# The second feed-forward's norm split in two: the gain in the matmul's operand, the token's factor on every up product

## The chip, the cores and the metric

The kernel runs on one core of a Trainium2 chip. The time is the device time of one execution in microseconds (us), lower being better. TensorE is PE in the profile, VectorE DVE, ScalarE ACT, GpSimd POOL, SyncE SP.

## The reference, cut to what matters

Two transformer blocks run one after the other on 256 tokens of width 1024, all in float32. The change touches only the end of the second one, its feed-forward on the residual `x`:

```python
def rms_norm(x, g):            # x / sqrt(mean(x*x) + eps) * g
...
h = rms_norm(x, norm_ffn_g[l])
u = causal_dwconv(h @ ffn_up[l], ffn_conv_w[l], ffn_conv_b[l])   # 3 taps along the tokens
u_gate, u_val = jnp.split(u, 2, axis=-1)                        # 2 x 2816 columns
x = x + (jax.nn.gelu(u_gate) * u_val) @ ffn_down[l]
return rms_norm(x, final_norm_g)
```

## The kernel before

Activations lie transposed: the 1024 features are 8 chunks `k` of 128 partitions, the 256 tokens lie along the free axis. So a gain (one number per feature) is a per-partition scalar, and a norm's factor (one number per token) is a row along the free axis, held on all partitions in `rstd`.

**Weights** stream as tiles of 128x1024 through a ring of four slots. For matmuls in parts, ScalarE copies each half tile (512 columns) rounded to the matmul's type into `w_parts` ("hi", the helper `tile_hi`, L1245), and VectorE subtracts that from the tile to get the rest ("lo", `part_lo`, L2249). A product is then three passes, hi*hi, hi*lo, lo*hi. `w_parts` holds four half tiles, so the hi of a half waits until TensorE has used the half four places earlier. SyncE loads the tile four places on once the lo of a tile is written.

**The output projection before the feed-forward** is 8 plain matmul tiles (L731), each followed on VectorE by the addition into `res` (L2243, semaphore `resid`) and on ScalarE by its square (L1487).

**The norm.** TensorE then sums the squares over the partitions with a matrix of ones (L741), ScalarE takes the root (L1045), VectorE the reciprocal (L1579, `inverse`) and scales all eight chunks by gain and factor into `h4T` (L1877, `norm`). ScalarE and VectorE split `h4T` into `h_parts` hi and lo, two chunks at a time (L1375, L2044). While this goes on TensorE turns the residual (L981) into the banks in which the down products accumulate later, and then waits for `h_lo`.

**The feed-forward** has 22 steps `f`, one for each 128 rows of the gate half and of the value half. On TensorE a step is `ffn_up(f)`, two products of 24 matmuls each (m = 0 gate, m = 1 value, L997), into banks 4 to 7 by turns, and `ffn_down(f - 1)` (12 matmuls, L1009). ScalarE reads a finished product from the bank, multiplies it by the last tap and adds the bias, each a per-partition scalar (`up_out`, L1508); VectorE adds the other two taps from the bank (`ff_taps`, L2264 and L2267), the second waiting for the first by a semaphore; ScalarE applies gelu (L1513); VectorE multiplies gate by value (`ff_gate`, L2273); ScalarE and VectorE split that (L1518 `act_parts`, L2278 `ff_lo`) for the down product. All engines run their programs strictly in the written order. The steps 2 to 17 run in a loop with registers on ScalarE and VectorE, four steps to an iteration; steps 1 and 18 to 21 are written out. A step of VectorE (before) is: gate(f-1), lo, lo, ff_lo(f-1), taps(f,0), lo, lo, taps(f,1), lo, lo. A step of ScalarE (`ff_step`) is:

```python
used(x, 0, i4); ahead(x, 0, i4)
used(x, 1, i4); act_parts(f - 1, i4); up_out(f, 0, i4); ahead(x, 1, i4)
used(x + 1, 0, i4); ahead(x + 1, 0, i4)
used(x + 1, 1, i4); up_out(f, 1, i4); ahead(x + 1, 1, i4); ff_gelu(f, i4)
used(x + 2, 0, i4); ahead(x + 2, 0, i4)
used(x + 2, 1, i4); ahead(x + 2, 1, i4)
```

Here `x = 3f - 1` is the tile of the gate product, x + 1 that of the value product, x + 2 that of down(f-1); `used(x, half)` waits until TensorE has used that half, and `ahead(x, half)` makes the hi of the same half of tile x + 2.

Of the kernel before, what the change touches and what calls it, by code (L numbers as in the profile page):

```python
# [14 lines left out]
F32 = mybir.dt.float32  # L15
F32R = mybir.dt.float32r
U32 = mybir.dt.uint32
ALU = mybir.AluOpType
# [53 lines left out]
rgw_in rg_in rg_conv_done rg_gates rg_sig rg_coeff rg_mult rg_ln rg_steps h3_ready rg_exp rg_pow rg_square lam_exp  # L72
logits2 probs2 maps2 o2_stat o2_root o2_ready ff_out ff_conv ff_taps ff_gelu ff_act final_done""".split()


def build(nc, wstream, x_t, cols_in, mats_in, mats1_in, matsa_in, crow_in, rows_in, out):
    ctx = ExitStack()
    with ctx:
# [215 lines left out]
        y2T = buf("y2T", KT, S)  # L294
        h4T = buf("h4T", KT, S)
        upp = buf("upp", 2, 2, S + 2)
        upc = buf("upc", 2, 2, S)
# [83 lines left out]
        def _(pe):  # L381
# [592 lines left out]
            for d in range(KT):  # L974
                full(N_OUT2 + d, y2T, 4 + d % 4, (sem["resid"], 2 * KT + d - 3) if d >= 4 else None)
            sum_squares2(4, sq3, 3)
            for tt in range(2):
                for d in range(KT):
                    if 2 * tt + d // 4 == 3:
                        pe.wait_ge(sem["roots"], 5)  # L980
                    pe.matmul(ps[:, 2 * tt + d // 4, P * (d % 4):P * (d % 4) + P], res[:, d, P * tt:P * tt + P], ident,  # L981
                              start=(d % 4 == 0), stop=False, is_transpose=True, skip_group_check=True)
            pe.wait_ge(sem["h_lo"], 16)

            def ffn_up(f, i4=0):

                for m in range(2):
                    if f >= 2:  # L990
                        pe.wait_ge(sem["ff_conv"], 2 * i4 + 2 * f - 3 + m)
                    x = max(3 * f - 1, 0) + m
                    for half in range(2):
                        pe.wait_ge(sem["w_lo"], 6 * i4 + 2 * (M_FFN + x) + half + 1)
                        for k in range(4):
                            for c, e in PASSES:
                                mm = pe.matmul(ps[:, 4 + 2 * (f % 2) + m, 0:S], w_parts[:, c, (2 * (M_FFN + x) + half) % 4, P * k:P * k + P],  # L997
                                               h_parts[:, e, 4 * half + k, :], start=(half == 0 and k == 0 and c + e == 0),
                                               stop=(half == 1 and k == 3 and c == 1))
                        mm.then_inc(sem["tiles_done" if half else "half_used"], 1)  # L1000

# [11 lines left out]

            ffn_up(0)
            ffn_up(1)
            ffn_down(0)
            with pe.Fori(0, (FT - 2) // 4) as i:
                for f in range(2, 6):
                    ffn_up(f, 4 * i)
                    ffn_down(f - 1, 4 * i)  # L1020
# [3 lines left out]
        def _(act):  # L1024
# [347 lines left out]

            def act_hi(src):
                for c in range(4):
                    act.activation(h_parts[:, 0, 2 * c:2 * c + 2, :], src[:, 2 * c:2 * c + 2, :], ACT.Copy).then_inc(sem["h_hi"], 1)  # L1375

            for k in range(KT):
# [113 lines left out]

            def used(x, half, i4=0):
# [68 lines left out]
        def _(dve):  # L1561
# [311 lines left out]

            def norm(r, dst, src, gain):
                inverse(r, S)
                for k in range(KT):
                    o = dve.scalar_tensor_tensor(dst[:, k, :], src[:, k, :], gain[:, k:k + 1], rstd[:, 0:S], ALU.mult, ALU.mult)  # L1877
                return o

            def route_query(h):  # L1880
# [158 lines left out]
            step(127, last=True)  # L2039
            def dve_lo(r, src):  # L2040

                for c in range(4):
                    dve.wait_ge(sem["h_hi"], 4 * r + c + 5)
                    dve.tensor_tensor(h_parts[:, 1, 2 * c:2 * c + 2, :], src[:, 2 * c:2 * c + 2, :],  # L2044
                                      h_parts[:, 0, 2 * c:2 * c + 2, :].bitcast(F32), ALU.subtract).then_inc(sem["h_lo"], 1)

            def in2_lo(t, half):
# [184 lines left out]
            for d in range(KT):  # L2232
                dve.wait_ge(sem["tiles_done"], N_BR2 + 2 * d + 2)
                b = 2 * (d % 2)
                y, t = y2T[:, d, :], fft[:, d % 2, :]
                dve.tensor_tensor(t, ps[:, b, 0:S], g2T[:, d, :], ALU.mult)
                link(dve.tensor_tensor(y, ps[:, b, S:2 * S], g2T[:, 16 + d, :], ALU.mult))
                link(dve.tensor_tensor(y, y, t, ALU.add))
                link(dve.tensor_tensor(t, ps[:, b + 1, 0:S], g2T[:, 8 + d, :], ALU.mult))
                dve.tensor_tensor(y, y, t, ALU.add).then_inc(sem["merged"], 1)  # L2240
            for d in range(KT):
                dve.wait_ge(sem["tiles_done"], N_OUT2 + d + 1)
                dve.tensor_tensor(res[:, d, :], ps[:, 4 + d % 4, 0:S], x2T[:, d, :], ALU.add).then_inc(sem["resid"], 1)  # L2243
            def part_lo(x, i4=0):

                for half in range(2):
                    h = 2 * (M_FFN + x) + half
                    dve.wait_ge(sem["w_hi"], 6 * i4 + h + 1)
                    dve.tensor_tensor(w_parts[:, 1, h % 4, :], ring[:, tile_of(M_FFN + x) % RING, 512 * half:512 * half + 512],  # L2249
                                      w_parts[:, 0, h % 4, :].bitcast(F32), ALU.subtract).then_inc(sem["w_lo"], 1)  # L2250

            for x in range(2):
                part_lo(x)
            norm(4, h4T, res, col("norm_ffn2")).then_inc(sem["normed"], 1)
            dve_lo(2, h4T)

            taps3 = col("ff_conv", 44, 3)

            def ff_taps(f, m, i4=0):

                bk, c = 4 + 2 * (f % 2) + m, bass.ds(i4 + f + FT * m, 1)
                dst = upc[:, f % 2, m, :]
                dve.wait_ge(sem["ff_out"], 2 * i4 + 2 * f + m + 1)
                dve.scalar_tensor_tensor(dst[:, 1:S], ps[:, bk, 0:S - 1], taps3[:, c, 1], dst[:, 1:S], ALU.mult, ALU.add  # L2264
                                         ).then_inc(sem["ff_taps"], 1)
                dve.wait_ge(sem["ff_taps"], 2 * i4 + 2 * f + m + 1)
                dve.scalar_tensor_tensor(dst[:, 2:S], ps[:, bk, 0:S - 2], taps3[:, c, 0], dst[:, 2:S], ALU.mult, ALU.add  # L2267
                                         ).then_inc(sem["ff_conv"], 1)
# [12 lines left out]
            def ff_step(f, i4=0):  # L2281

                ff_gate(f - 1, i4)
                part_lo(3 * f + 1, i4)
                ff_lo(f - 1, i4)
                ff_taps(f, 0, i4)
                part_lo(3 * f + 2, i4)
                ff_taps(f, 1, i4)
                if 3 * f + 3 < 3 * FT:
                    part_lo(3 * f + 3, i4)  # L2290

            for m in range(2):
                part_lo(2 + m)
                ff_taps(0, m)
# [220 lines left out]
```

## Time and profile before

| | us |
|---|---|
| median of 3 runs (lowest, highest) | 1961.96 (1959.88, 1962.26) |
| the profiled execution, its own time | 1961.08 |
| its span in the trace | 1959.3 |
| TensorE busy | 1828.5 (93%) |
| VectorE busy | 1232.5 (63%) |
| ScalarE busy | 993.5 (51%) |

The span runs from the first to the last instruction; what lies around it is 1.8 us. All times below are counted from the span's start. The stage that the change touches runs from about 1744.9 us (last projection tile through) to the end.

### The profile page before, as it was taken

The page shows a single profiled execution, that of the slowest core. Times are in us where ns is not written, and L with a number is a line of the kernel's source. Part 1 is how long each engine was busy: PE and PEld are TensorE (multiplying, and loading weights), DVE is VectorE, ACT ScalarE, POOL GpSimd, SP SyncE. Part 2 cuts the span into 40 slices and gives each one's busy share as a digit, 9 for nine tenths or more (in the row PEclk, how much of TensorE's full clock was granted, in tenths as well). Part 3 has the DMA queues.
Part 4 walks back from the last instruction along what each step waited for, and adds up shares of the span by engine and source line. Part 5 has one row for each costly group of instructions (what it writes and reads, how often), then busy time and mean ns, then how long its engine had stood idle before and what let it go on. Part 6 is the DMA issues. An engine that isn't in the chain of part 4 may idle for free.

```text
span 1959.3 us, 34312 instructions
## 1 busy us (share of the span) xinstructions
PE 1828.5 (93%) x11798; PEld 1639.1 (84%) x11798; DVE 1232.5 (63%) x2463; ACT 993.5 (51%) x1986; POOL 148.7 (8%) x118
## 2 busy tenths in 40 slices
PE   7899989998999986799999999999899997989997
PEld 1777879998889976688899999999899886879997
DVE  1685356555178979866666666666776664237776
ACT  2545523241136668766555555555558555016665
POOL 0000003330044720000000000000000000000000
PEclk9899969898999999999999999999999998999999
DMA  7423212122445530155555555555354432435553
GB/s 263 176 99 98 93 59 97 65 74 99 150 152 173 181 127 1 36 192 194 190 192 182 187 187 187 188 183 192 138 178 158 147 112 82 154 129 180 182 182 120
DMA packets 77267, 283.28 MB, mean 145 GB/s; under 512 B 8576, under 2 KB 8576, under 8 KB 76928
## 3 DMA queue, kind: packets, MB, share of 16 engines
q1 hardware_dynamic: 77184, 282.16, 42.2%
q8 instruction: 53, 0.87, 0.2%
q14 instruction: 30, 0.25, 0.0%
HBM read 281.08 MB, written 1.05 MB: 144 GB/s over the span
## 4 chain that ended last, share of the span: by engine, by line
PE 83%; DVE 11%; ACT 4%; issue 1%; DMA 1%; POOL 1%; POOLq 0%; SPq 0%; DVEq 0%; ACTq 0%
PE banks L802 18%; PE banks L790 16%; PE banks L864 8%; PE banks L427 7%; PE banks L997 6%; PE banks L731 4%; PE banks L1009 3%; PE banks L602 2%; PE banks L586 2%; DVE split L1979 2%; PE banks L969 1%; PE banks L754 1%; DVE arena L1977 1%; PE banks L400 1%; PE banks L591 1%
## 5 line engine op out<-in xcount | busy, mean ns | idle before, releaser
L1264 ACT ACTIVATE split<-arena 128x512 fp32r<-128x512 f32 x508 | 318.9, 629 | 145.4 <-PE banks L790 83.1
L790 PEld LDWEIGHTS banks<-split 128*128 128x128 f32 x3072 | 379.5, 192 | 11.1 <-DVE split L1916 3.1
L790 PE MATMUL banks<-split 128*128 128x256 f32 x3072 | 383.0, 283 | 3.1 <-DVE split L1916 2.2
L802 PE MATMUL banks<-split 128*128 128x512 f32 x1536 | 363.4, 390 | 2.7 <-issue 2.7
L1993 DVE TENSOR_TENSOR split<-arena,split 128x512 fp32r<-128x512 f32 x412 | 281.8, 690 | 115.8 <-ACT split L1264 110.1
L802 PEld LDWEIGHTS banks<-split 128*128 128x128 f32 x1536 | 283.3, 188 | 58.4 <-issue 2.9
L1245 ACT ACTIVATE split<-arena 128x512 fp32r<-128x512 f32 x264 | 163.9, 626 | 84.8 <-PE banks L864 29.8
L864 PE MATMUL banks<-split 128*128 128x256 f32 x1344 | 169.3, 286 | 4.0 <-DVE split L2075 3.9
L864 PEld LDWEIGHTS banks<-split 128*128 128x128 f32 x1344 | 164.7, 193 | 7.6 <-issue 5.9
L427 PE MATMUL banks<-split 128*128 128x256 f32 (+2 forms) x936 | 155.1, 329 | 7.5 <-DVE split L1585 6.5
L427 PEld LDWEIGHTS banks<-split 128*128 128x128 f32 (+1 forms) x936 | 138.4, 202 | 25.9 <-issue 8.3
L997 PEld LDWEIGHTS banks<-split 128*128 128x128 f32 x1056 | 131.1, 194 | 8.9 <-DVE split L2044 7.3
L997 PE MATMUL banks<-split 128*128 128x256 f32 x1056 | 131.7, 285 | 7.1 <-DVE split L2044 7.1
L2052 DVE TENSOR_TENSOR split<-arena,split 128x512 fp32r<-128x512 f32 x128 | 87.2, 689 | 70.6 <-ACT split L1245 69.2
L2249 DVE TENSOR_TENSOR split<-arena,split 128x512 fp32r<-128x512 f32 x132 | 89.1, 688 | 46.8 <-ACT split L1245 45.2
L828 PE MATMUL banks<-split,arena 128*128 128x128 f32 x512 | 66.1, 284 | 32.3 <-DVE arena L1982 32.3
L2377 POOL TENSOR_TENSOR split<-arena,split 128x512 fp32r<-128x512 f32 x68 | 90.7, 1362 | 71.9 <-DVE split L1916 51.2
L828 PEld LDWEIGHTS banks<-split,arena 128*128 128x128 f32 x512 | 61.1, 196 | 37.4 <-DVE split L1979 33.4
L731 PE MATMUL banks<-arena 128*128 128x256 f32 x384 | 84.7, 380 | 3.7 <-DVE arena L2240 2.2
L1585 DVE TENSOR_TENSOR split<-arena,split 128x512 fp32r<-128x512 f32 x78 | 53.1, 690 | 54.2 <-ACT split L1052 53.8
L731 PEld LDWEIGHTS banks<-arena 128*128 128x128 f32 x384 | 72.8, 190 | 14.3 <-DVE arena L2240 2.6
L2009 DVE TENSOR_TENSOR arena<-arena 128x256 f32<-128x256 f32 x80 | 49.1, 614 | 45.0 <-ACT arena L1326 44.9
(372 smaller groups left out, 2384.1 us busy)
## 6 DMA issues: line engine op xcount, KB each, us to landing
arena<-wstream SPq DMA_DIRECT2D x525, 512.0 KB, 3.2
arena<-x_t SPq DMA_DIRECT2D x1, 2048.0 KB, 13.4
arena<-matsa SPq DMA_DIRECT2D x1, 1234.0 KB, 6.3
out_t<-arena SPq DMA_DIRECT2D x4, 256.0 KB, 2.1
arena<-mats SPq DMA_DIRECT2D x1, 576.0 KB, 8.0
arena<-crow SPq DMA_DIRECT2D x1, 512.0 KB, 7.1
arena<-rows SPq DMA_DIRECT2D x1, 512.0 KB, 4.4
arena<-mats SPq DMA_DIRECT2D x1, 449.0 KB, 5.5
```

What stands on the lines that cost most here:

```text
L427: mm = pe.matmul(ps[0:rows, b, 0:m], w_parts[:, c, (2 * t + k // 4) % 4, P * (k % 4):P * (k % 4) + rows], hp[:, e, k, 0:m], start=(k == 0 ...
L731: mm = pe.matmul(ps[:, b, 0:S], w[:, P * k:P * k + P], src[:, k, :], start=(k == 0), stop=(k == KT - 1))
L790: mm = pe.matmul(ps[:, 4 + b, 0:S], w_parts[:, c, (2 * m + half) % 4, P * k:P * k + P], h_parts[:, e, 4 * half + k, :], start=(half == 0 a ...
L802: mm = pe.matmul(ps[:, 2 * tt + half, :], g_parts[:, e, j % 2, P * tt:P * tt + P], w_parts[:, c, (2 * m + half) % 4, :], start=(first and ...
L828: pe.matmul(ps[:, W_BANKS[g % 3] + t // 4, P * (t % 4):P * (t % 4) + P], hot1[g % 2][:, t, :], hot2[:, g % 2, t, :].bitcast(F32), start=Tr ...
L864: mm = pe.matmul(out, w_parts[:, c, (2 * m + half) % 4, P * k:P * k + P], src[:, e, 4 * half + k, :], start=(half == 0 and k == 0 and c + ...
L997: mm = pe.matmul(ps[:, 4 + 2 * (f % 2) + m, 0:S], w_parts[:, c, (2 * (M_FFN + x) + half) % 4, P * k:P * k + P], h_parts[:, e, 4 * half + k ...
L1245: act.activation(w_parts[:, 0, h % 4, :], ring[:, slot, 512 * half:512 * half + 512], ACT.Copy).then_inc(sem["w_hi"], 1)
L1264: act.activation(w_parts[:, 0, (2 * m + half) % 4, :], ring[:, peer_slot(m), 512 * half:512 * half + 512], ACT.Copy).then_inc(sem["w_hi"], 1)
L1993: dve.tensor_tensor(w_parts[:, 1, (2 * m + half) % 4, :], ring[:, slot, 512 * half:512 * half + 512], w_parts[:, 0, (2 * m + half) % 4, :] ...
L2249: dve.tensor_tensor(w_parts[:, 1, h % 4, :], ring[:, tile_of(M_FFN + x) % RING, 512 * half:512 * half + 512], w_parts[:, 0, h % 4, :].bitc ...
L2377: pool.tensor_tensor(w_parts[:, 1, (2 * m + half) % 4, :], ring[:, (N_PEER + m) % RING, 512 * half:512 * half + 512], w_parts[:, 0, (2 * m ...
```

## The change: what it does

The gain is put into the matmul's operand without waiting for the factor, chunk by chunk as the residual is made: ScalarE writes hi = `res * gain` into `h_parts` (an Identity activation with the gain as scale), VectorE writes lo = `res * gain - hi` (`weighted_lo`). `h4T`, `norm`, `act_hi` and `dve_lo` are gone. The factor, which is the same for all features of a token, is put on each finished up product by a new VectorE operation `ff_norm`, from the bank into a buffer `upn`; `up_out` and both taps read `upn` in place of the bank. `up_out` now waits for `ff_norm`, and TensorE's reuse of a bank waits for `ff_norm` of two steps back rather than for the taps. TensorE's order becomes: first up product, sums of squares, second up product, turning of the residual, both products of step 1.

```diff
# TensorE
-            sum_squares2(4, sq3, 3)
-            for tt in range(2):
+            def turn_residual(tt):
...
-            pe.wait_ge(sem["h_lo"], 16)
...
+            def ffn_up(f, m, i4=0):
+                if f >= 2:
+                    pe.wait_ge(sem["ff_norm"], 2 * i4 + 2 * f - 3 + m)
+                x = max(3 * f - 1, 0) + m
+                if x == 0:
+                    pe.wait_ge(sem["resid"], 2 * KT + 5)
+                for half in range(2):
+                    pe.wait_ge(sem["w_lo"], 6 * i4 + 2 * (M_FFN + x) + half + 1)
+                    for k in range(4):
+                        if x == 0:
+                            pe.wait_ge(sem["h_lo"], 12 + 4 * half + k + 1)
...
-            ffn_up(0)
-            ffn_up(1)
+            ffn_up(0, 0)
+            sum_squares2(4, sq3, 3)
+            ffn_up(0, 1)
+            for tt in range(2):
+                turn_residual(tt)
+            for m in range(2):
+                ffn_up(1, m)
# ScalarE
                 act.wait_ge(sem["resid"], 2 * KT + k + 1)
+                act.activation(h_parts[:, 0, k, :], res[:, k, :], ACT.Identity, scale=col("norm_ffn2")[:, k:k + 1]).then_inc(sem["h_hi"], 1)
                 act.activation(sq3[:, k, :], res[:, k, :], ACT.Square).then_inc(sem["squares"], 1)
-            roots(4, S, 3)
-            act.wait_ge(sem["normed"], 2)
-            act_hi(h4T)
...
                 c = bass.ds(i4 + f + FT * m, 1)
-                act.activation(upc[:, f % 2, m, :], ps[:, 4 + 2 * (f % 2) + m, 0:S], ACT.Identity, scale=last_tap[:, c],
+                act.wait_ge(sem["ff_norm"], 2 * i4 + 2 * f + m + 1)
+                act.activation(upc[:, f % 2, m, :], upn[:, f % 2, m, :], ACT.Identity, scale=last_tap[:, c],
                                bias=col("ff_conv_b")[:, c]).then_inc(sem["ff_out"], 1)
...
             for x in range(2):
                 for half in range(2):
                     used(x, half)
-                    if half:
-                        up_out(0, x)
                     ahead(x, half)
+                if x == 0:
+                    roots(4, S, 3)
+            for m in range(2):
+                up_out(0, m)
             ff_gelu(0)
# VectorE
+            def weighted_lo(k):
+                dve.wait_ge(sem["h_hi"], 12 + k + 1)
+                dve.scalar_tensor_tensor(h_parts[:, 1, k, :], res[:, k, :], col("norm_ffn2")[:, k:k + 1], h_parts[:, 0, k, :].bitcast(F32),
+                                         ALU.mult, ALU.subtract).then_inc(sem["h_lo"], 1)
             for d in range(KT):
                 dve.wait_ge(sem["tiles_done"], N_OUT2 + d + 1)
                 dve.tensor_tensor(res[:, d, :], ps[:, 4 + d % 4, 0:S], x2T[:, d, :], ALU.add).then_inc(sem["resid"], 1)
+                if d:
+                    weighted_lo(d - 1)
+                if d == 6:
+                    for half in range(2):
+                        part_lo(0, half)
+            weighted_lo(KT - 1)
+            for x in (1, 2):
                 for half in range(2):
+                    part_lo(x, half)
+            inverse(4, S)
...
-            norm(4, h4T, res, col("norm_ffn2")).then_inc(sem["normed"], 1)
-            dve_lo(2, h4T)
...
+            def ff_norm(f, m, i4=0):
+                dve.wait_ge(sem["tiles_done"], 3 * i4 + N_FFN + max(3 * f - 1, 0) + m + 1)
+                dve.tensor_tensor(upn[:, f % 2, m, :], ps[:, 4 + 2 * (f % 2) + m, 0:S], rstd[:, 0:S], ALU.mult).then_inc(sem["ff_norm"], 1)
...
             def ff_step(f, i4=0):
                 ff_gate(f - 1, i4)
-                part_lo(3 * f + 1, i4)
+                part_lo(3 * f + 1, 0, i4)
+                ff_norm(f, 0, i4)
                 ff_lo(f - 1, i4)
+                part_lo(3 * f + 1, 1, i4)
                 ff_taps(f, 0, i4)
-                part_lo(3 * f + 2, i4)
+                part_lo(3 * f + 2, 0, i4)
+                ff_norm(f, 1, i4)
+                part_lo(3 * f + 2, 1, i4)
                 ff_taps(f, 1, i4)
                 if 3 * f + 3 < 3 * FT:
-                    part_lo(3 * f + 3, i4)
+                    for half in range(2):
+                        part_lo(3 * f + 3, half, i4)
 
             for m in range(2):
-                part_lo(2 + m)
+                ff_norm(0, m)
+            for half in range(2):
+                part_lo(3, half)
+            for m in range(2):
                 ff_taps(0, m)
```

## Rows read from the trace of the kernel before

**Rows 1.** The page: busy times, and the chain that ended last by engine.
```profile
PE 1828.5 (93%) x11798; PEld 1639.1 (84%) x11798; DVE 1232.5 (63%) x2463; ACT 993.5 (51%) x1986; POOL 148.7 (8%) x118
PE 83%; DVE 11%; ACT 4%; issue 1%; DMA 1%; POOL 1%; POOLq 0%; SPq 0%; DVEq 0%; ACTq 0%
```
**Rows 2.** Windows: stretch, us, busy PE, PEld, DVE, ACT, POOL, PE clock, DMA, GB/s.
```profile
1773.98:1911.09 137.11, 137.11 (x963) 129.06 (x962) 100.54 (x192) 83.07 (x160) 0.00 (x0) 1.00 0.54 184
1748.00:1757.30 9.30, 2.23 (x19) 1.89 (x17) 7.51 (x13) 2.66 (x5) 0.00 (x0) 0.85 0.45 162
1757.30:1761.30 4.00, 3.99 (x18) 3.99 (x19) 0.36 (x1) 0.63 (x1) 0.00 (x0) 0.50 0.00 0
740.00:800.00 60.00, 40.74 (x323) 37.32 (x321) 60.00 (x101) 49.36 (x143) 0.00 (x0) 1.00 0.00 1
```
**Rows 3.** The chain that ended last, in order of time: start us, us, what.
```profile
1745.02 3.47 PE banks L741 x16
...
1749.02 1.76 DVE arena L1579
...
1750.81 3.27 DVE arena L1877 x8
...
1754.76 2.51 DVE split L2044 x4
...
1757.31 7.76 PE banks L997 x48
...
1773.98 5.75 PE banks L997 x48
1779.73 2.84 PE banks L1009 x12
...
1842.56 5.75 PE banks L997 x48
...
1936.62 5.77 PE banks L997 x48
...
1946.71 3.07 PE banks L1009 x12
```
**Rows 4.** Timeline of a loop step on ACT: start us, us, operation [idle before].
```profile
1848.56 0.57 ACT L1508 ACTIVATE arena<-banks,arena 128x256 f32<-128x256 f32 x1 [1.02 <-PE banks L997]
1849.03 0.62 ACT L1245 ACTIVATE split<-arena 128x512 fp32r<-128x512 f32 x1
...
1852.59 0.63 ACT L1245 ACTIVATE split<-arena 128x512 fp32r<-128x512 f32 x1 [0.80 <-PE banks L997]
```
**Rows 5.** The same timeline on DVE.
```profile
1850.29 0.48 DVE L2264 SCALAR_TENSOR_TENSOR arena<-banks,arena 128x255 f32<-128x255 f32 x1
1850.91 0.48 DVE L2267 SCALAR_TENSOR_TENSOR arena<-banks,arena 128x254 f32<-128x254 f32 x1
1851.31 1.28 DVE L2249 TENSOR_TENSOR split<-arena,split 128x512 fp32r<-128x512 f32 x2
1852.51 0.42 DVE L2273 TENSOR_TENSOR arena<-arena 128x256 f32<-128x256 f32 x1
1853.26 0.69 DVE L2249 TENSOR_TENSOR split<-arena,split 128x512 fp32r<-128x512 f32 x1 [0.33 <-ACT split L1245]
```
**Rows 6.** Groups by line and shape: line, engine, tiles, count | busy us, mean ns | idle before.
```profile
L1508 ACT ACTIVATE arena<-banks,arena 128x256 f32<-128x256 f32 x44 | 24.5, 557 | 21.8 <-PE banks L997 21.8
L1402 ACT ACTIVATE arena<-banks,arena 128x256 f32<-128x256 f32 x24 | 11.3, 472 | 20.6 <-PE banks L864 20.6
L1487 ACT ACTIVATE arena<-arena 128x256 f32<-128x256 f32 x8 | 3.3, 416 | 81.2 <-DVE arena L2243 81.2
L1235 ACT ACTIVATE arena<-arena 128x256 f32<-128x256 f32 x8 | 4.1, 508 | 58.0 <-DVE arena L1871 58.0
L2243 DVE TENSOR_TENSOR arena<-banks,arena 128x256 f32<-128x256 f32 x8 | 3.4, 425 | 25.0 <-PE banks L731 25.0
L1877 DVE SCALAR_TENSOR_TENSOR arena<-arena 128x256 f32<-128x256 f32 x8 | 3.3, 480 | 0.0
```

More of the change, by code:

```diff
@@ L72 @@
 rgw_in rg_in rg_conv_done rg_gates rg_sig rg_coeff rg_mult rg_ln rg_steps h3_ready rg_exp rg_pow rg_square lam_exp
-logits2 probs2 maps2 o2_stat o2_root o2_ready ff_out ff_conv ff_taps ff_gelu ff_act final_done""".split()
+logits2 probs2 maps2 o2_stat o2_root o2_ready ff_norm ff_out ff_conv ff_taps ff_gelu ff_act final_done""".split()
 def build(nc, wstream, x_t, cols_in, mats_in, mats1_in, matsa_in, crow_in, rows_in, out):
@@ L294, in build @@
         y2T = buf("y2T", KT, S)
-        h4T = buf("h4T", KT, S)
-        upp = buf("upp", 2, 2, S + 2)
+        upn = buf("upn", 2, 2, S)
         upc = buf("upc", 2, 2, S)
@@ L982, in _ @@
                               start=(d % 4 == 0), stop=False, is_transpose=True, skip_group_check=True)
-            pe.wait_ge(sem["h_lo"], 16)
[L987 to L1000, printed above, removed]
+            def ffn_up(f, m, i4=0):
[9 more added lines that the diff above has]
+                            pe.wait_ge(sem["h_lo"], 12 + 4 * half + k + 1)
+                        for c, e in PASSES:
+                            mm = pe.matmul(ps[:, 4 + 2 * (f % 2) + m, 0:S], w_parts[:, c, (2 * (M_FFN + x) + half) % 4, P * k:P * k + P],
+                                           h_parts[:, e, 4 * half + k, :], start=(half == 0 and k == 0 and c + e == 0),
+                                           stop=(half == 1 and k == 3 and c == 1))
+                    mm.then_inc(sem["tiles_done" if half else "half_used"], 1)
             def ffn_down(f, i4=0, x=None, last=False):
@@ L1018, in _ @@
                 for f in range(2, 6):
-                    ffn_up(f, 4 * i)
+                    for m in range(2):
+                        ffn_up(f, m, 4 * i)
                     ffn_down(f - 1, 4 * i)
@@ L1371, in part_hi @@
                 tile_hi(n % RING, 12 * i4 + 16 * (n // RING + 1), half, 2 * m + half)
-            def act_hi(src):
-                for c in range(4):
-                    act.activation(h_parts[:, 0, 2 * c:2 * c + 2, :], src[:, 2 * c:2 * c + 2, :], ACT.Copy).then_inc(sem["h_hi"], 1)
             for k in range(KT):
@@ L1872, in _ @@
                                          ALU.mult, ALU.add).then_inc(sem["resid"], 1)
[L1874 to L1878, printed above, removed]
             def route_query(h):
@@ L2039, in _ @@
             step(127, last=True)
[L2040 to L2045, printed above, removed]
             def in2_lo(t, half):
@@ L2240, in _, with part_lo @@
                 dve.tensor_tensor(y, y, t, ALU.add).then_inc(sem["merged"], 1)
+            def part_lo(x, half, i4=0):
+                h = 2 * (M_FFN + x) + half
+                dve.wait_ge(sem["w_hi"], 6 * i4 + h + 1)
+                dve.tensor_tensor(w_parts[:, 1, h % 4, :], ring[:, tile_of(M_FFN + x) % RING, 512 * half:512 * half + 512],
+                                  w_parts[:, 0, h % 4, :].bitcast(F32), ALU.subtract).then_inc(sem["w_lo"], 1)
+            def weighted_lo(k):
+                dve.wait_ge(sem["h_hi"], 12 + k + 1)
+                dve.scalar_tensor_tensor(h_parts[:, 1, k, :], res[:, k, :], col("norm_ffn2")[:, k:k + 1], h_parts[:, 0, k, :].bitcast(F32),
+                                         ALU.mult, ALU.subtract).then_inc(sem["h_lo"], 1)
             for d in range(KT):
@@ L2243, in _ @@
                 dve.tensor_tensor(res[:, d, :], ps[:, 4 + d % 4, 0:S], x2T[:, d, :], ALU.add).then_inc(sem["resid"], 1)
-            def part_lo(x, i4=0):
-                for half in range(2):
[L2247 to L2250, printed above, removed]
@@ L2252, in _ @@
-            for x in range(2):
-                part_lo(x)
-            norm(4, h4T, res, col("norm_ffn2")).then_inc(sem["normed"], 1)
-            dve_lo(2, h4T)
+                if d:
[5 more added lines that the diff above has]
+            for x in (1, 2):
+                for half in range(2):
+                    part_lo(x, half)
+            inverse(4, S)
@@ L2257, in _ @@
             taps3 = col("ff_conv", 44, 3)
+            def ff_norm(f, m, i4=0):
+                dve.wait_ge(sem["tiles_done"], 3 * i4 + N_FFN + max(3 * f - 1, 0) + m + 1)
+                dve.tensor_tensor(upn[:, f % 2, m, :], ps[:, 4 + 2 * (f % 2) + m, 0:S], rstd[:, 0:S], ALU.mult).then_inc(sem["ff_norm"], 1)
             def ff_taps(f, m, i4=0):
-                bk, c = 4 + 2 * (f % 2) + m, bass.ds(i4 + f + FT * m, 1)
-                dst = upc[:, f % 2, m, :]
+                c = bass.ds(i4 + f + FT * m, 1)
+                src, dst = upn[:, f % 2, m, :], upc[:, f % 2, m, :]
@@ L2263, in ff_taps @@
                 dve.wait_ge(sem["ff_out"], 2 * i4 + 2 * f + m + 1)
-                dve.scalar_tensor_tensor(dst[:, 1:S], ps[:, bk, 0:S - 1], taps3[:, c, 1], dst[:, 1:S], ALU.mult, ALU.add
+                dve.scalar_tensor_tensor(dst[:, 1:S], src[:, 0:S - 1], taps3[:, c, 1], dst[:, 1:S], ALU.mult, ALU.add
                                          ).then_inc(sem["ff_taps"], 1)
                 dve.wait_ge(sem["ff_taps"], 2 * i4 + 2 * f + m + 1)
-                dve.scalar_tensor_tensor(dst[:, 2:S], ps[:, bk, 0:S - 2], taps3[:, c, 0], dst[:, 2:S], ALU.mult, ALU.add
+                dve.scalar_tensor_tensor(dst[:, 2:S], src[:, 0:S - 2], taps3[:, c, 0], dst[:, 2:S], ALU.mult, ALU.add
@@ L2283, in ff_step @@
                 ff_gate(f - 1, i4)
-                part_lo(3 * f + 1, i4)
+                part_lo(3 * f + 1, 0, i4)
+                ff_norm(f, 0, i4)
                 ff_lo(f - 1, i4)
+                part_lo(3 * f + 1, 1, i4)
                 ff_taps(f, 0, i4)
-                part_lo(3 * f + 2, i4)
+                part_lo(3 * f + 2, 0, i4)
+                ff_norm(f, 1, i4)
+                part_lo(3 * f + 2, 1, i4)
                 ff_taps(f, 1, i4)
                 if 3 * f + 3 < 3 * FT:
-                    part_lo(3 * f + 3, i4)
+                    for half in range(2):
+                        part_lo(3 * f + 3, half, i4)
             for m in range(2):
-                part_lo(2 + m)
+                ff_norm(0, m)
+            for half in range(2):
+                part_lo(3, half)
+            for m in range(2):
                 ff_taps(0, m)
```

## The prediction

> **What bounds the kernel now.** I read the page first: TensorE is busy 93% of the span, and the chain of waits that ended last is TensorE for 83% [rows 1]. So time is won only where TensorE stands still, and lost only where something makes it stand still. Then I looked at the feed-forward by windows and along the chain. Two stretches differ. In the first, from 1748.0 to 1757.3 us, TensorE is busy 2.23 of 9.30 us, and behind it runs at a granted clock of 0.50 [rows 2], that is at 1.2 in place of 2.4 GHz. The chain leaves it in this stretch: root, reciprocal (1.76 us), eight scalings (3.27), splits (2.51) [rows 3]. In the second, the loop, TensorE is busy 137.11 of 137.11 us at clock 1.00, and the chain is nothing but up products (5.75 us) and down products (2.8 us); 16 steps take 137.11 us, 8.57 each. VectorE is busy 100.54 us there (73%), ScalarE 83.07 (61%) [rows 2, 3]. The change takes work out of the first stretch and puts work on the two other engines in the second.
>
> **Part 1, the start.** TensorE's idle time of 9.30 - 2.23 = 7.07 us goes, since the first up product needs only residual chunks, each split a few tenths after it is made. Will they be there? The last chunk is added by 1745.5; hi (0.51) and lo (0.48) follow, done by 1746.5; TensorE starts the product at 1744.9 and reaches that chunk 2.5 us later. The sums then come 2.87 us later than before, reciprocal included until 1753.7, and two up products, the sums and the turning (some 11 us) cover them. With the idle time goes the slow clock behind it: from 1757.31 to 1773.98 the chain has four products and a down product, which at the loop's pace are 4 x 2.875 + 2.83 = 14.33 us and took 16.67 [rows 3], so 2.3 us more. Laid out in the new order, TensorE begins step 2 at 1764.7 in place of 1773.98: **9.3 us gained**. The extra ScalarE and VectorE operations per projection tile (1 each, about 0.5 us in a period of 3.4) hide under its matmuls, and the loads keep their order: SyncE's next load waits for a lo that is now made earlier, and POOL's queue has nothing in this stage.
>
> **Part 2, the loop.** Counted by busy time nothing happens: ff_norm is a tensor-tensor from a bank, 0.425 us as L2243 [rows 6]; two per step bring VectorE from 6.28 to 7.13 of 8.57 us. But busy time is not what decides here. ff_norm stands ahead of up_out, up_out stands in ScalarE's order ahead of a hi, and VectorE's own next operation is the lo of that hi. Both engines work in order, so twice per step VectorE stands still through a round trip over ScalarE. Before, up_out waited only for TensorE, and the lo's had slack. So I add the ring in which each operation can only start when the one before allows:
>
> - ff_norm 0.425, up to its end [rows 6].
> - From there to up_out. In the loop this operation computes its scalar addresses from registers after its wait: the product of step 10 ends on the chain at 1842.56 + 5.75 = 1848.31 and up_out starts at 1848.56, 0.25 later; in the written-out step 21 the product ends at 1942.39 and the chain goes on 0.02 later [rows 3, 4]. I take 0.26.
> - up_out itself, as far as it holds up the next operation. Bounds: 0.32 to 0.51. From a bank it takes 0.557 with two scalars (scale and bias), L1402 with one takes 0.472; out of SBUF no scalar takes 0.416 (L1487) and one takes 0.508 (L1235) [rows 6]. So a scalar costs 0.09, SBUF as source 0.036 more than a bank, and two scalars out of SBUF come to 0.60. The next operation starts 0.10 ahead of the end (1848.56 to 1849.03 at 0.57) [rows 4]: 0.51, the value nearest in form. The low end is the row without scalars.
> - hi 0.62, and 0.03 until the lo starts (1852.59 + 0.63 to 1853.26) [rows 4, 5].
>
> One round trip is 1.85, two are 3.69. The rest of the ring is VectorE's own work, start to start: six lo's at 0.60 (two L2249 from 1851.31 to 1852.51) = 3.62; twice the first tap to the second, 0.62 (1850.29 to 1850.91), = 1.24; twice the second tap, 0.40, = 0.80; the gate, 0.34 (its 0.42 less the 0.08 by which the others overlap) [rows 5]. ff_lo lies inside the wait for the hi. **The ring is 9.69 us against 8.57.** The taps read SBUF now. Bounds for one: 0.42, which is what L2273 takes on SBUF alone in another operation [rows 5], and the 0.48 of today. I leave them at 0.48, since L1877 is the same operation on SBUF alone and takes 0.480 [rows 6].
>
> The Trainium skill says otherwise on that point: "VectorE: DVE Perf Modes", section on the TRN2 errata, gives VectorE 58 cycles plus the elements at 0.96 GHz out of SBUF and 120 out of PSUM, so a tap would be some 65 ns cheaper, an estimate from that page. By it the ring would be 9.43; the trace, with 480 ns from either side, does not agree.
>
> In the written-out steps 18 to 21 there is no register work: 0.23 less per round trip and about 0.1 less per pair of taps, a ring of 9.02, still over TensorE's 8.5.
>
> **The sum.** I lay the operations out one by one with these durations. Gate of step 0 falls at 1757.8; step 1's ring and a short wait for its product put gate 1 at 1767.15. At that time VectorE still has slack: TensorE needs its step 2 from 1764.7 on and the splits are two half tiles ahead; this is used up within two steps, after which TensorE waits about 1.1 us per step for a lo. Gate 17 is at 1767.15 + 16 x 9.69 = 1922.2, gate 20 at +3 x 9.02 = 1949.3. Gate 21 follows after 9.02 less the two lo's of a tile that does not exist (1.2), then gate, hi and lo of the gated product (0.42 each, 0.2 between) and the down product, 3.07 [rows 3]: last matmul at 1961.6. Before it is 1946.71 + 3.07 = 1949.78 [rows 3]. The rest (final norm, output) is unchanged. **Sum: +11.8 us**, being -9.3 at the start, about +18 in the steps and +3 at the tail, where TensorE now waits longer for the last gated product. On the profiled execution's own 1961.08 that is 1972.9. That execution lies between the lowest and highest of the three runs and 0.9 below their median, so I take 1973.
>
> **The rivals.**
> B, the register work is done ahead of the wait. For: sequencers do some of it early elsewhere. Against: the 0.25 us before up_out, where the wait comes first, as it would here. The ring is 9.24 and the end 7 us earlier: 1966.
> C, the taps get cheaper once they leave the bank, down to the low end: 0.06 each, four per step, 0.24 off the ring, 20 steps, 5 us less: 1968. For: a bank is a different source, and ScalarE shows 0.036 between the two. Against: L1877 [rows 6]. The rule of the Trainium skill above is this rival.
> D, the other side, faster: TensorE stays the bound. Place: the two round trips of the loop. It decides for this when the ring is under 8.57, that is, if the round trips overlap VectorE's own work rather than follow it, which leaves the 7.13 of busy time. For: 73% plus 10% occupancy. Against: program order; the lo right behind each round trip cannot be made earlier, and only ff_lo is between. Then the start's gain stays, less some 0.8 at the tail: 1961.08 - 9.3 + 0.8 = 1952.6.
> M, a mixture: low ends throughout (up_out at 0.33, part of the register work hidden) give a ring near 9.1: between 1958 and 1965, no change that can be told.
> E, the clock falls in TensorE's new pauses. The clock fell once behind an idle stretch of 7 us, but from 740 to 800 us TensorE is busy only 68% and keeps 1.00 [rows 2], and pauses here are 1.1 us at a time. Each fall like the one at the start costs about 2.3 us; two to four of them give 1978 to 1982.
> G, the change does not do what it says: the first product still waits for the last chunk or a load. All of part 1 except a little is gone: 1980.
>
> **How the numbers follow.** The forecast 0.60, B 0.10, C 0.06, D 0.09, M 0.05, E 0.08, G 0.02. The range from 1965 to 1979 takes in the forecast with its bounds (ring 9.55 to 9.85, 3 us each way), B, C and half of E; D, M, G and the rest of E, 0.2, are outside. A measurement of this kernel tells 0.2% (3.9 us) from no change. Faster: D, 0.09. Within: M, 0.05. Slower: the rest, 0.86.
>
> **What would show it.** Right: no idle time of TensorE and no clock below 1.00 between 1745 and 1765, step 2 begins near 1764.7; in the loop, steps of 9.7 us with TensorE waiting about 1.1 us for a lo and VectorE twice about 1.2 us for ScalarE's hi; up_out at 0.60. Steps of 9.2 to 9.5 mean B or C (look at the time from ff_norm's end to up_out, and at the taps' duration). Wrong altogether: steps of 8.57 with no wait on lo, or clock stretches at 0.50 inside the loop, or TensorE idle before its first up product.

## The result and the profile after

The changed kernel takes 1975.16 us (median of 6 runs, 1968.87 to 1979.09) against 1962.03 before (6 runs, 1959.44 to 1965.45). The ratio is 1.0064, 95% interval 1.0046 to 1.0082: slower by 0.6%. Forecast: 1973, range 1965 to 1979.

The profiled execution took 1979.09 us, its span is 1977.0. It is 18 us above the profiled one of before, but 4.4 us of that lie in front of the stage that was changed: its first matmul starts at 1749.23 instead of 1744.86. Up to there TensorE runs the same program in both kernels. The gap between the same matmul groups is 1.3 us at 214 us of before's time, 5.2 at 313, and 4.5 from 383 us on; at the stage's start it is 4.4, so the operations added to each projection tile cost nothing. It comes with the granted clock: in the first 320 us the changed kernel's execution has it at half speed for 61.5 us, that of before for 51.3 (added up from the trace in windows of 4 us). I therefore compare **the stage**, from its first matmul behind the projection to the end of the last one: 1749.23 to 1967.46, that is 218.2 us, against 204.9 before. That is +13.3; forecast +11.8.

The start, in the timeline of the changed kernel (start us, us, engine, line, operation, count, idle before):

```profile
1749.23 3.21 PE L995 MATMUL banks<-split 128*128 128x256 f32 x24
...
1752.28 3.62 PE L740 MATMUL banks<-arena 128*128 128x256 f32 x16
...
1755.55 3.23 PE L995 MATMUL banks<-split 128*128 128x256 f32 x24
...
1758.61 1.91 PE L979 MATMUL banks<-arena 128*128 128x128 f32 x16
...
1760.28 6.00 PE L995 MATMUL banks<-split 128*128 128x256 f32 x48
...
1766.12 2.91 PE L1007 MATMUL banks<-split 128*128 128x512 f32 x12
...
1768.86 5.92 PE L995 MATMUL banks<-split 128*128 128x256 f32 x48
```

One matmul group follows the other without idle time. Step 2 starts 1768.86 - 1749.23 = 19.63 us into the stage; before it was 1773.82 - 1744.86 = 28.96, so 9.3 us are gained. The windows say the same of the clock, which was 0.50 behind the idle stretch of before [rows 2], and show the price in the loop (columns as in [rows 2]):

```profile
1749.20:1768.86 19.66, 19.66 (x142) 18.73 (x141) 13.76 (x26) 10.26 (x19) 0.00 (x0) 1.00 0.56 189
1788.84:1922.00 133.16, 123.88 (x831) 111.64 (x832) 95.70 (x195) 69.00 (x137) 0.00 (x0) 1.00 0.49 164
1958.60:1962.80 4.20, 0.14 (x1) 0.00 (x0) 2.42 (x5) 1.76 (x4) 0.00 (x0) 1.00 0.00 0
1963.80:1967.40 3.60, 3.60 (x10) 2.38 (x8) 0.00 (x0) 0.00 (x0) 0.00 (x0) 0.53 0.00 0
```

In the loop TensorE is now busy 123.88 of 133.16 us where it had no idle time, and VectorE, at 72%, is not busy all the time either. So neither engine is full: the time goes into waits in a circle. One step of it, VectorE first, then ScalarE:

```profile
1781.28 0.42 DVE L2275 TENSOR_TENSOR arena<-arena 128x256 f32<-128x256 f32 x1
1781.61 0.68 DVE L2232 TENSOR_TENSOR split<-arena,split 128x512 fp32r<-128x512 f32 x1
...
1782.21 0.42 DVE L2259 TENSOR_TENSOR arena<-banks,arena 128x256 f32<-128x256 f32 x1
1782.55 0.41 DVE L2280 TENSOR_TENSOR split<-arena,split 128x256 fp32r<-128x256 f32 x1
...
1784.04 0.69 DVE L2232 TENSOR_TENSOR split<-arena,split 128x512 fp32r<-128x512 f32 x1 [1.07 <-ACT split L1249]
...
1786.27 0.42 DVE L2259 TENSOR_TENSOR arena<-banks,arena 128x256 f32<-128x256 f32 x1
1786.54 1.59 PE L995 MATMUL banks<-split 128*128 128x256 f32 x12
...
1788.09 0.69 DVE L2232 TENSOR_TENSOR split<-arena,split 128x512 fp32r<-128x512 f32 x1 [1.40 <-ACT split L1249]
...
1788.84 4.77 PE L995 MATMUL banks<-split 128*128 128x256 f32 x36 [0.71 <-DVE split L2232]
...
1790.93 0.42 DVE L2275 TENSOR_TENSOR arena<-arena 128x256 f32<-128x256 f32 x1
```
```profile
1782.88 0.60 ACT L1506 ACTIVATE arena<-arena 128x256 f32<-128x256 f32 x1 [0.73 <-DVE arena L2259]
1783.39 1.14 ACT L1249 ACTIVATE split<-arena 128x512 fp32r<-128x512 f32 x2
1786.94 0.60 ACT L1506 ACTIVATE arena<-arena 128x256 f32<-128x256 f32 x1 [2.41 <-PE banks L1007]
1787.44 0.62 ACT L1249 ACTIVATE split<-arena 128x512 fp32r<-128x512 f32 x1
```

Follow the round trip: ff_norm (L2259) ends at 1786.27 + 0.42 = 1786.69; up_out (L1506) starts 0.25 later; the hi behind it (L1249) 0.50 after that; VectorE's lo (L2232) starts at 1788.09, having waited 1.40 us; TensorE has waited for that lo too. From gate (L2275) to gate it is 1790.93 - 1781.28 = 9.65 us. That is 1.15 us more than 8.50, TensorE's own time for a step; 0.71 of it shows as idle time in front of L995, the other 0.44 is in the records on both sides of that wait, which take 1.59 and 4.77 us for 48 matmuls where step 2 takes 5.92. A caution on reading: the second up_out names "PE banks L1007" as what ended its wait. That is the releaser the profile inferred; the down product merely ended at about the same time. The first up_out, in the same place of the program, names L2259, and the 0.25 us behind ff_norm's end are the same both times.

### The profile page after: what moved, and what is told of

It reads as the page before. It is cut to its first block, busy times and chain, and to the rows that moved or that the text cites. A ratio compares the mean times of both kernels' runs of the same rounds, so it can differ in the third digit from the quotient of the medians.

```text
span 1977.0 us, 34413 instructions
## 1 busy us (share of the span) xinstructions
PE 1837.3 (93%) x11798; PEld 1641.4 (83%) x11798; DVE 1243.3 (63%) x2503; ACT 993.1 (50%) x1990; POOL 148.8 (8%) x118
## 4 chain that ended last, share of the span: by engine, by line
PE 74%; DVE 15%; ACT 5%; issue 4%; DMA 1%; POOL 1%; DVEq 0%; ACTq 0%; POOLq 0%; SPq 0%
PE banks L801 18%; PE banks L789 16%; PE banks L863 8%; PE banks L426 7%; PE banks L730 4%; PE banks L601 2%; DVE split L2232 2%; PE banks L585 2%; DVE split L1973 2%; ACT split L1249 2%; PE banks L968 1%; PE banks L753 1%; DVE arena L1971 1%; PE banks L399 1%; DVE arena L2266 1%
## 5 line engine op out<-in xcount | busy, mean ns | idle before, releaser
L1268 ACT ACTIVATE split<-arena 128x512 fp32r<-128x512 f32 x508 | 319.4, 630 | 145.1 <-PE banks L789 83.1
L789 PE MATMUL banks<-split 128*128 128x256 f32 x3072 | 383.0, 283 | 3.2 <-DVE split L1910 2.3
L1249 ACT ACTIVATE split<-arena 128x512 fp32r<-128x512 f32 x264 | 157.5, 622 | 53.0 <-PE banks L863 29.7
L863 PE MATMUL banks<-split 128*128 128x256 f32 x1344 | 169.3, 286 | 4.0 <-DVE split L2062 3.9
L995 PE MATMUL banks<-split 128*128 128x256 f32 x1056 | 138.8, 286 | 11.7 <-DVE split L2232 11.7
L995 PEld LDWEIGHTS banks<-split 128*128 128x128 f32 x1056 | 130.7, 191 | 20.3 <-DVE split L2232 15.5
L2232 DVE TENSOR_TENSOR split<-arena,split 128x512 fp32r<-128x512 f32 x132 | 88.8, 688 | 50.3 <-ACT split L1249 50.3
## 6 DMA issues: line engine op xcount, KB each, us to landing
arena<-x_t SPq DMA_DIRECT2D x1, 2048.0 KB, 13.1
```

Of the source, the lines that this page charges most:

```text
L789: mm = pe.matmul(ps[:, 4 + b, 0:S], w_parts[:, c, (2 * m + half) % 4, P * k:P * k + P], h_parts[:, e, 4 * half + k, :], start=(half == 0 a ...
L863: mm = pe.matmul(out, w_parts[:, c, (2 * m + half) % 4, P * k:P * k + P], src[:, e, 4 * half + k, :], start=(half == 0 and k == 0 and c + ...
L1249: act.activation(w_parts[:, 0, h % 4, :], ring[:, slot, 512 * half:512 * half + 512], ACT.Copy).then_inc(sem["w_hi"], 1)
L1268: act.activation(w_parts[:, 0, (2 * m + half) % 4, :], ring[:, peer_slot(m), 512 * half:512 * half + 512], ACT.Copy).then_inc(sem["w_hi"], 1)
```

## The experiments

All rest on the changed kernel unless said otherwise. "Steps" is the distance between the starts of the down products of neighbouring loop steps. Experiment 1 has seven executions; each of the others has one, so they are compared by the steps and the stage of that execution, which stay clear of what happens to the clock before the stage. A table of all runs closes the section.

**1. The hi in front of up_out.**

```diff
                 act_parts(f - 1, i4)
+                ahead(x, 1, i4)
                 up_out(f, 0, i4)
-                ahead(x, 1, i4)
...
+                ahead(x + 1, 1, i4)
                 up_out(f, 1, i4)
-                ahead(x + 1, 1, i4)
```

> Edit: the changed kernel, with one line moved twice on ScalarE: the hi of the next half tile (ahead) stands in front of up_out instead of behind it, for the gate and for the value product. No instruction more or less. Theory 1 (the ring: VectorE waits twice per step for a hi that stands in ScalarE's order behind up_out, which waits for ff_norm): the ring is broken, steps go back to TensorE's 8.57 us from 9.65, the start's gain of 9.3 us stays, and the time is about 9 us below before, near 1952 (ratio to before 0.995). Theory 2 (VectorE's and ScalarE's added work, or contention for the memory, is what slows the steps): the same work is done, so steps stay within 0.1 us of 9.65 and the time near 1974. Theory 3 (the register work and semaphore traffic of the added waits on TensorE's side): steps stay at 9.65 as well.

Measured: 1950.94 us (median of 7 runs, 1945.04 to 1957.33) against 1961.6 of before beside it (12 runs); ratio 0.9945, interval 0.9924 to 0.9967. The timeline of TensorE's down products and the windows:

```profile
1866.82 2.91 PE L1007 MATMUL banks<-split 128*128 128x512 f32 x12
...
1875.32 2.91 PE L1007 MATMUL banks<-split 128*128 128x512 f32 x12
```
```profile
1764.00:1900.00 136.00, 136.00 (x963) 128.14 (x962) 115.02 (x225) 85.55 (x161) 0.00 (x0) 1.00 0.55 185
```

Steps are 8.50 us (why not 8.57, see experiment 9), TensorE has no idle time, and VectorE is busy 85% where it was 72%. The same instructions in another order: theory 1 holds, 2 and 3 fall. The stage takes 194.0 us, 24.2 less than the changed kernel and 10.9 less than before. This is the version that beats both kernels.

**2 and 3. Two spare products on VectorE, inside the waits or outside them.** The operation is the same in both kernels, `dve.tensor_tensor(spare, rstd[:, 0:S], rstd[:, 0:S], ALU.mult)`.

```diff
# 2: in the waits
                 ff_lo(f - 1, i4)
+                spare product
...
                 ff_norm(f, 1, i4)
+                spare product
# 3: behind the taps
                 ff_taps(f, 0, i4)
+                spare product
...
                 ff_taps(f, 1, i4)
+                spare product
```

> Edit: the changed kernel plus two spare VectorE products of 128x256 per step (0.42 us each), one behind ff_lo and one behind the second ff_norm, that is at the places where VectorE waits for ScalarE's hi. Theory 1 (the ring) says that they fall into waits of some 1.1 and 1.4 us: steps stay at 9.65 us (within 0.03). Theory 2 (VectorE's amount of work decides) says at least 2 x 0.34 more: steps of 10.3 us, 11 us more in the time.

> Edit: the same two spare VectorE products per step, but behind the two pairs of taps, where VectorE does not wait. Theory 1 (the ring) says they lengthen it by 2 x 0.34: steps of 10.33 us, some 14 us over the 20 steps. Theory 2 (the amount of work) says the same as for the kernel with the spare products in the waits; the two kernels have the same instructions, so a difference between them is the place alone.

Down products of two neighbouring steps, first with the products in the waits, then behind the taps:

```profile
1867.92 2.91 PE L1008 MATMUL banks<-split 128*128 128x512 f32 x12
...
1877.58 2.91 PE L1008 MATMUL banks<-split 128*128 128x512 f32 x12
```
```profile
1867.46 2.91 PE L1008 MATMUL banks<-split 128*128 128x512 f32 x12
...
1877.78 2.91 PE L1008 MATMUL banks<-split 128*128 128x512 f32 x12
```

9.66 against 10.32 us: in the waits the same work is free, on the ring it costs 0.67 per step, twice its start-to-start time of 0.33. The stages are 217.9 and 232.3 us (changed kernel 218.2): -0.4 and +14.1. With the same instructions in both kernels, it is their place that costs and not their amount.

**4. The same with the ring broken.** Kernel 1 with the spare products where kernel 3 has them.

> Edit: the kernel with hi first, plus the two spare VectorE products of 128x256 per step behind the taps, where they cost 0.67 us per step in the changed kernel. Theory 1 (only the ring made VectorE's order decide): with the ring broken VectorE's own work, about 7.1 us, leaves 1.4 us of slack per step, the two products (0.67) fit and steps stay at 8.50 us. Theory 2 (amount of work decides as soon as it grows): steps of 9.2 us.

```profile
1868.78 2.91 PE L1008 MATMUL banks<-split 128*128 128x512 f32 x12
...
1877.28 2.91 PE L1008 MATMUL banks<-split 128*128 128x512 f32 x12
```

8.50 us; the stage takes 194.5. From 1790 to 1910 us VectorE is busy 108.34 of 120 us (90%) and TensorE all 120. What cost 14 us in experiment 3 is free here.

**5. Only the value product's hi in front.** The second of the two moves of experiment 1 alone.

> Edit: the changed kernel with the hi in front of up_out for the value product alone; the gate product's round trip stays. The ring theory with one round trip in place of two: the ring is below TensorE's own time (9.65 less about 1.2), steps of 8.50 to 8.65 us. A theory in which each wait costs by itself, whatever else the engines do, says half of the loss stays: about 9.1 us.

The first seven distances are 8.50, the eighth 8.54, while VectorE's lead lasts; then they settle at 8.66 (down products at 1862.38, 1871.04 and 1879.71); the stage takes 197.7. That is a touch over the upper end of what the ring theory gave, and far from 9.1. The rows tell why 8.66: with the hi out of the way VectorE's next wait is for up_out itself, whose end lets the taps start.

```profile
1856.21 0.41 DVE L2259 TENSOR_TENSOR arena<-banks,arena 128x256 f32<-128x256 f32 x1
1856.54 0.68 DVE L2232 TENSOR_TENSOR split<-arena,split 128x512 fp32r<-128x512 f32 x1
1857.64 0.48 DVE L2266 SCALAR_TENSOR_TENSOR arena<-arena 128x255 f32<-128x255 f32 x1 [0.42 <-ACT arena L1506]
```

From ff_norm to the first tap it is 1.43 us; in the changed kernel it is 1788.70 - 1786.27 = 2.43 (the round trip and a lo). 9.65 - 1.00 = 8.65. With both moved it would be some 7.65 (an estimate from these rows), which is below TensorE's 8.50.

**6. Loops written out.**

```diff
-            with act.Fori(0, (FT - 2) // 4 - 1) as i:
-                for f in range(2, 6):
-                    ff_step(f, 4 * i)
-            for f in range(FT - 4, FT):
+            for f in range(2, FT):
                 ff_step(f)
```

(and the same on VectorE)

> Edit: the changed kernel with the loops of steps 2 to 17 on ScalarE and VectorE written out with constants (TensorE keeps its loop), so that up_out and the taps compute no address in registers behind their waits. By the prediction's terms each round trip loses 0.22 us and each pair of taps 0.11: the ring is 9.02 instead of 9.69, as in steps 18 to 21 of the changed kernel, 16 x 0.65 = some 10 us less in all. If register work is done ahead of the wait, or fetching the longer code costs as much, steps stay near 9.65.

Steps are 9.07 us (down products at 1861.00, 1870.06, 1879.14), as predicted to 0.05; the stage takes 208.7, 9.5 less. ff_norm ends at 1850.36 + 0.42 = 1850.78 there, and ScalarE's timeline has up_out 0.03 us behind it instead of 0.25, its wait 0.46 us instead of 0.73:

```profile
1850.81 0.60 ACT L1506 ACTIVATE arena<-arena 128x256 f32<-128x256 f32 x1 [0.46 <-DVE arena L2256]
```

**7. up_out as a plain copy** (the last tap and the bias left out).

```diff
-act.activation(upc[...], upn[...], ACT.Identity, scale=last_tap[:, c], bias=col("ff_conv_b")[:, c])
+act.activation(upc[...], upn[...], ACT.Copy)
```

> Edit: the changed kernel with up_out as a plain copy. Left out of the computation: the last tap and the bias. The prediction's term for up_out (0.51 us as far as it holds up the hi, from 0.32 without scalars plus 0.09 for each) gives a ring shorter by 2 x 0.18 = 0.36: steps of 9.3 us in the loop; there the address work of the two scalars goes too, so up to 2 x 0.22 more is possible, 8.85. In the written-out steps 18 to 21, which have no address work, 9.06 - 0.36 = 8.70. If the scalars cost nothing there, 9.06.

```profile
1850.12 0.42 ACT L1506 ACTIVATE arena<-arena 128x256 f32<-128x256 f32 x1 [0.52 <-DVE arena L2258]
1850.44 1.14 ACT L1249 ACTIVATE split<-arena 128x512 fp32r<-128x512 f32 x2
```

The copy takes 0.42 in place of 0.60 and holds the hi up by 0.32 in place of 0.51; steps are 8.85 in the loop (9.65 - 0.36 - 0.44) and 8.69 in steps 18 to 21. Both terms of up_out had the size that was given them. The wait in ScalarE's row is 0.2 shorter as well. VectorE's row beside it tells why:

```profile
1849.67 0.42 DVE L2258 TENSOR_TENSOR arena<-banks,arena 128x256 f32<-128x256 f32 x1
```

ff_norm ends at 1850.09 and the copy starts 0.03 us later, in a loop that still has its registers for everything else. So it is the addresses of the two scalars that took the 0.22 us. Experiment 6 says the same.

**8. No factor** (the norm's factor on the up products left out): no ff_norm, up_out and taps on the bank, TensorE waits for the taps.

> Edit: the changed kernel without ff_norm: up_out and the taps read the bank as before, TensorE waits for the taps as before. Left out of the computation: the token's factor on the up products. What stays is the start alone. By the prediction's split, 9.3 us are gained at the start and nothing is lost in the steps: they are at 8.57 us or, as in the kernel with hi first, at 8.50, and the stage from the last projection tile to the last matmul is 10 to 11 us shorter than before's 204.9 us (194 to 195). If the start's gain were part of a trade (the earlier start itself slowing the steps, for instance by loads that come too late), steps would stay above 8.6.

Steps are 8.50 (1862.22, 1870.72, 1879.22) and the stage takes 194.4 us, 10.5 less than before. By parts: the first down product starts 16.88 us into the stage instead of 26.11 (9.2 gained), the 20 distances between the first 21 down products sum to 170.0 instead of 171.2 (the 0.07 us of experiment 9), and the tail is the same. The start gains what it was said to gain and costs the loop nothing.

**9. The kernel before, with ff_lo earlier.**

```diff
-                part_lo(3 * f + 1, i4)
+                part_lo(3 * f + 1, i4, (0,))
                 ff_lo(f - 1, i4)
+                part_lo(3 * f + 1, i4, (1,))
```

> Edit: the kernel before, with VectorE's ff_lo between the two lo's of the down tile instead of behind both. It is about the 0.07 us by which the loop steps of before (8.57) are longer than those of the kernel with hi first (8.50). In before the weights of the first down matmul, which are the gated product's parts, are loaded 0.03 us ahead of it, in the changed kernel 0.12 us. Theory a: TensorE waits 0.07 us per step there for ff_lo, so with an earlier ff_lo steps are 8.50 us. Theory b: the 0.07 come from TensorE's wait for the taps of two steps back or from the bank's reader, and steps stay at 8.57.

```profile
1848.69 2.60 PEld L1009 LDWEIGHTS banks<-split 128*128 128x128 f32 x12
1848.81 2.91 PE L1009 MATMUL banks<-split 128*128 128x512 f32 x12
```

The same two rows in the kernel before:

```profile
1865.25 2.58 PEld L1009 LDWEIGHTS banks<-split 128*128 128x128 f32 x12
1865.28 2.98 PE L1009 MATMUL banks<-split 128*128 128x512 f32 x12
```

With ff_lo earlier the weights are loaded 0.12 us ahead instead of 0.03, the down product takes 2.91 us instead of 2.98, and steps are 8.50 (1865.81, 1874.31): theory a. The stage is 204.15, 0.75 shorter. The 20 distances between the first 21 down products give 1.2 of that (170.0 against 171.2). But the first of them came 0.5 us later in its stage than before: the clock behind the idle stretch stayed at 0.50 for 5.9 us in this execution (1758.14 to about 1764.0) and for 4.0 in that of before (1757.31 to about 1761.3). A gain of this size does not show in one execution's time (1961.16 beside 1959.92).

**All runs side by side.** Times in us. "Before" is the kernel before, run beside this one. The last two columns are TensorE's idle time in front of the last down product and that product's duration.

| kernel | time (executions) | before | stage | loop step | idle | last product |
|---|---|---|---|---|---|---|
| before | 1961.96 (3) | | 204.9 | 8.57 | 1.57 | 3.06 |
| changed | 1975.16 (6) | 1962.03 | 218.2 | 9.65 | 4.12 | 4.61 |
| 1, hi first | 1950.94 (7) | 1961.6 | 194.0 | 8.50 | 1.18 | 3.03 |
| 2, spare products in the waits | 1975.78 (1) | 1961.6 | 217.9 | 9.65 | 4.10 | 4.39 |
| 3, spare products behind the taps | 1992.69 (1) | 1961.6 | 232.3 | 10.32 | 4.57 | 4.96 |
| 4, hi first and spare products | 1955.67 (1) | 1971.84 | 194.5 | 8.50 | 1.65 | 3.01 |
| 5, hi first for the value only | 1951.99 (1) | 1959.92 | 197.7 | 8.66 | 1.81 | 4.62 |
| 6, loops written out | 1965.53 (1) | 1961.6 | 208.7 | 9.07 | 4.09 | 4.60 |
| 7, plain copy | 1963.08 (1) | 1959.92 | 204.3 | 8.85 | 3.71 | 5.49 |
| 8, no factor | 1949.06 (1) | 1959.92 | 194.4 | 8.50 | 1.59 | 3.02 |
| 9, before with ff_lo earlier | 1961.16 (1) | 1959.92 | 204.2 | 8.50 | 1.58 | 3.04 |

## Why the prediction was right

**The start.** Forecast 9.3 us, measured 9.3; the slow clock went with the idle time, and experiment 8 has the gain by itself. That rules out rival G as well.

**The ring.** Forecast 9.69 in the loop and 9.02 in the written-out steps; measured 9.65 and 9.07. Term by term: round trip 1.85 forecast, 1.82 and 1.83 in the rows; up_out's duration 0.60 forecast, 0.604 the median of 44; its hold on the hi 0.51 against 0.50 to 0.51; register work 0.26 against 0.25, and shown by its absence (experiment 6); scalars 2 x 0.09, shown by theirs (experiment 7). TensorE's wait of about 1.1 us per step came as 1.15, of which 0.71 shows as idle time. That the waits are in series, which was the claim that decided between the forecast and rival D, is shown by experiments 1 to 4: an order in which they are not in series takes 24 us off with the same work.

**Rival B**, register work ahead of the wait, is out: 0.25 us are there and go with the loop. **Rival C**, cheaper taps out of SBUF, is out: L2266 has a median of 479 ns on SBUF against 476 for L2264 on the bank. So the trace disagrees here with the Trainium skill, "VectorE: DVE Perf Modes", section on the TRN2 errata, by which a tap would have been some 65 ns cheaper, an estimate from that page. **Rival E**, the clock, did not come in the loop (1.00 in the window above, with TensorE idle 7% of it). It did come once, at the end. **Rival M**, low ends throughout with a ring near 9.1, is out with 9.65.

**The tail.** This term was mis-sized. I costed the last down product at its 3.07 us of before [rows 3]. In the changed kernel TensorE waits longer in front of it, as forecast, and then runs it at a granted clock of 0.53:

```profile
1955.83 2.91 PE L1007 MATMUL banks<-split 128*128 128x512 f32 x12
1962.85 4.61 PE L1007 MATMUL banks<-split 128*128 128x512 f32 x12 [4.12 <-DVE split L2280]
```

Behind 4.12 us of idle time it took 4.61 us; in before, behind 1.57 us, 3.07. Those 1.5 us are the difference between +13.3 and +11.8: the forecast has the last product start 213.7 us into the stage (1961.6 - 3.07 - 1744.86), and it started at 213.6. The wait in front of it grew by 2.5 us, near the forecast's 3; the 16 + 4 steps cost 18.5 against 18.

What lets the clock fall there is not settled. Over the eleven kernels the product is slow behind pauses of 3.71 to 4.57 us and at its usual 3.0 to 3.1 behind pauses of 1.18 to 1.65. But in experiment 5 it took 4.62 us behind 1.81 us only, with TensorE busy all the time from 1900 to 1934 us:

```profile
1935.90 4.62 PE L1007 MATMUL banks<-split 128*128 128x512 f32 x12 [1.81 <-DVE split L2280]
```

And the slowest product (5.49, experiment 7) does not have the longest pause. A longer pause goes with the fall in these rows, but the pause alone was not tried by itself, and in the loop, where TensorE pauses 0.71 us in each step, the clock stayed at 1.00.

**The level.** 1973 was forecast from the one execution at 1961.08; the stage's +13.3 on it gives 1974.4, against a median of 1975.16. Medians compared with medians say the same (+13.1). Single executions of the changed kernel lie 10 us apart, so that the forecast came within 2.2 us of the median is in part luck; what bears the forecast out is the stage and its steps, term by term.

## What to carry to other kernels

Busy shares do not tell what an added operation costs when two in-order engines feed each other: write down the ring (each operation's start to the next start it allows, over both engines, waits and address work included) and compare it with the bound engine's period. If the ring is longer, look first for an operation that stands in program order behind the new wait without needing it, and move it in front; here one line moved twice turned +0.6% into -0.55%. A spare operation put inside and outside the suspected wait tells a ring from a full engine with two runs.

## What the runs showed of the hardware that was not expected

- An activation or vector operation whose scalar operands are addressed by registers starts later after a wait than one with fixed addresses: 0.25 us against 0.03 on ScalarE with two such scalars (experiments 6 and 7). In the changed kernel the trace has register operations of ScalarE's queue, 35 to 74 ns each, at 1782.7 and 1786.8 us, that is between ff_norm's end and up_out. On VectorE the second tap starts 0.62 us behind the first in the loop and 0.51 in the written-out kernel. It cost nothing where the engine did not wait: in experiment 1 up_out starts 0.52 us behind the hi in front of it, as back to back operations do.

```profile
1847.54 0.61 ACT L1249 ACTIVATE split<-arena 128x512 fp32r<-128x512 f32 x1
1848.06 0.59 ACT L1506 ACTIVATE arena<-arena 128x256 f32<-128x256 f32 x1
```

- The loop of the kernel before lost 0.07 us per step because the gated product's lo, part of the operand that the down matmuls load as weights, came late: the load ran 0.03 us ahead of the first matmul instead of 0.12, and an earlier ff_lo gave the 0.07 us back (experiment 9). TensorE's busy share does not show it (137.11 of 137.11 us) [rows 2].
- The same program takes up to 10 us more or less before this stage begins (first matmul of the stage at 1739.42 to 1749.89 us over eleven profiled executions). It goes with how long the clock is granted at half speed before the stage: 88 us from 0 to 1740 in the one that got there first, 99 in that of before, 106 in that of the changed kernel, 116 in the one that came last (added up from windows of 4 and 10 us). Most of the spread lies in the first 320 us (47.7 to 61.5 us), but not all: the one that came last has 54.6 there and loses its time behind 1390 us. For effects of a few us in one stage, the stage's own length is the better measure.
